# Four of 336 expert weight loads issued as sixteen transfers of eight partitions each

## What is computed

```
def moe_swiglu(h, router_w, router_b, w1, w3, w2):
    logits = (h @ router_w).astype(jnp.float32) + router_b.astype(jnp.float32)
    top_val, top_idx = lax.top_k(logits, TOP_K)
    top_p = jax.nn.softmax(top_val, axis=-1)
    combine = jnp.sum(jax.nn.one_hot(top_idx, N_EXPERTS, dtype=jnp.float32) * top_p[..., None], axis=-2)
    out = jnp.zeros_like(h)
    for e in range(N_EXPERTS):
        out = out + combine[..., e:e + 1].astype(h.dtype) * swiglu(h, w1[e], w3[e], w2[e])
    return out
```

## Time and profile before

| | us |
|---|---|
| median of 3 runs | 1876.97 (1876.92 to 1880.12) |
| profiled execution, its own time | 1879.21 |
| its span, first to last instruction | 1877.3 |
| TensorE busy (PE) | 1807.9 |
| VectorE, ScalarE, GpSimd busy | 601.2, 447.2, 409.4 |
| bytes moved by DMA | 506.40 MB |
| expert slabs issued | 336, between 987.0 and 1828.3 |
| mean granted TensorE clock | 0.992 |

### The profile page before, as it was taken

The page is one execution under the profiler, slowest core; times in us unless marked ns, Lnnn a source line. Parts: engine busy times, 40 slices in busy tenths (PEclk is TensorE's granted clock), DMA queues, the critical chain, the costliest instruction groups (busy, mean ns, idle before and its releaser), DMA issues.

```text
span 1877.3 us, 45084 instructions
## 1 busy us (share of the span) xinstructions
PE 1807.9 (96%) x20352; PEld 1325.0 (71%) x20353; DVE 601.2 (32%) x1199; ACT 447.2 (24%) x740; POOL 409.4 (22%) x126
## 2 busy tenths in 40 slices
PE   6999999999999999999999999999999889999986
PEld 4875788898888888995997566666665456666543
DVE  4356133243362454557555112021111111020112
ACT  4347423234212222527443000000000000000001
POOL 2410434445546545421552000000000000000000
PEclk8999999999999999999999999999999999999999
DMA  8352222234443474340459999999999999999993
GB/s 355 138 202 91 93 108 95 90 112 180 153 183 137 164 282 180 114 156 4 178 180 378 413 376 408 419 419 419 419 419 419 419 419 420 418 419 419 418 417 156
DMA packets 70133, 506.40 MB, mean 270 GB/s; under 512 B 7792, under 2 KB 8048, under 8 KB 9264
## 3 DMA queue, kind: packets, MB, share of 16 engines
q1 hardware_dynamic: 69552, 501.09, 66.3%
q0 software_dynamic: 384, 2.36, 0.3%
HBM read 502.37 MB, written 1.05 MB: 268 GB/s over the span
## 4 chain that ended last, share of the span: by engine, by line
PE 72%; issue 10%; DMA 6%; POOL 5%; SPq 5%; DVE 1%; ACT 1%; DVEq 0%; POOLq 0%; ACTq 0%
PE bank L1575 22%; PE bank L987 11%; PE bank L988 11%; PE bank L989 11%; PE bank L1599 9%; POOL w_lo L618 5%; SPq L845 5%; DMA moe_slab<-in_moe_w 3%; PE bank L1587 2%; DMA moe_slab<-in_moe_up 1%; DMA start_slab<-in_w_mod 1%; PE pv_bank L1338 1%; PE turned_pair L1320 1%; PE bank L1022 1%; PE bank L1296 1%
## 5 line engine op out<-in xcount | busy, mean ns | idle before, releaser
L1575 PE MATMUL bank<-moe_slab,HE 128*32 128x256 f32 x9408 | 527.3, 381 | 17.5 <-DMA moe_slab<-in_moe_up 14.2
L618 POOL TENSOR_TENSOR w_lo<-slab,w_hi 128x2048 fp32r<-128x2048 f32 (+3 forms) x88 | 369.0, 4195 | 541.2 <-ACT w_hi L1813 541.1
L1575 PEld LDWEIGHTS bank<-moe_slab,HE 128*32 128x32 f32 x9408 | 306.8, 110 | 224.8 <-DMA moe_slab<-in_moe_up 16.7
L987 PE MATMUL bank<-H_HI,w_hi 128*128 128x512 f32 (+1 forms) x912 | 321.1, 352 | 0.1
L988 PE MATMUL bank<-H_LO,w_hi 128*128 128x512 f32 (+1 forms) x912 | 319.2, 350 | 0.0
L989 PE MATMUL bank<-H_HI,w_lo 128*128 128x512 f32 (+1 forms) x912 | 319.1, 350 | 0.0
L1813 ACT ACTIVATE w_hi<-slab 128x2048 fp32r<-128x2048 f32 (+1 forms) x88 | 165.8, 1889 | 142.0 <-PE bank L989 142.0
L987 PEld LDWEIGHTS bank<-H_HI,w_hi 128*128 128x128 f32 x912 | 172.4, 189 | 26.5 <-POOL w_lo L618 1.9
L949 POOL TENSOR_TENSOR OUT<-OUT,RINVF 128x256 f32<-128x256 f32 x2 | 1.6, 813 | 864.5 <-DVE RINVF L3126 864.5
L989 PEld LDWEIGHTS bank<-H_HI,w_lo 128*128 128x128 f32 x912 | 172.5, 189 | 22.7
L988 PEld LDWEIGHTS bank<-H_LO,w_hi 128*128 128x128 f32 x912 | 172.5, 189 | 22.0
(11 more groups left out here) (316 smaller groups left out, 2123.9 us busy)
## 6 DMA issues: line engine op xcount, KB each, us to landing
moe_slab<-in_moe_up SPq DMA_DIRECT2D x224, 1024.0 KB, 26.8
moe_slab<-in_moe_w SPq DMA_DIRECT2D x112, 1024.0 KB, 27.1
slab<-in_w_in SPq DMA_DIRECT2D x38, 1024.0 KB, 4.8
slab<-in_ffn_w SPq DMA_DIRECT2D x30, 1024.0 KB, 4.8
row_slab<-in_w_mod_rows SPq DMA_DIRECT2D x28, 1024.0 KB, 7.1
start_slab<-in_w_mod SPq DMA_DIRECT2D x8, 1024.0 KB, 17.5
slab<-in_w_proj SPq DMA_DIRECT2D x8, 1024.0 KB, 4.8
slab<-in_w_out SPq DMA_DIRECT2D x8, 1024.0 KB, 4.8
```

The source lines that it names most:

```text
L618: engine.tensor_tensor(lo, raw, hi.bitcast(F32), ALU.subtract).then_inc(done, 1)
L987: mm(out, lhs[0], rhs[0], start=start, stop=False)
L1575: ins = mm(outs[t // 2][32 * b:32 * b + 32, 256 * (t % 2):256 * (t % 2) + 256], rows[t], w[:, 256 * b:256 * b + 256], start=first and t != ...
```

## The change

Slabs 84, 148, 212 and 276 are loaded as sixteen transfers of eight partitions each, one after the other, in place of one transfer of 128. All four go to buffer 4. Each of the sixteen adds 16 to the buffer's semaphore, so such a slab adds 256, and a table made beforehand, `SLAB_IN`, gives TensorE the count to wait for. `wait_expert_slab` gets the same correction. All other loads, their order and their waits stay.

```diff
--- before.py
+++ after.py
@@ -339,6 +339,14 @@
 STREAM += [("down", STEPS - 1, _i) for _i in range(2)]
 STREAM_AT = {k: n for n, k in enumerate(STREAM)}
 assert len(STREAM) == N_EXPERTS * N_EXPERT_SLABS
+
+
+SIXTEENTHS_AT = (84, 148, 212, 276)
+HOME_COUNT = [0] * MOE_RING
+SLAB_IN = []
+for _k in range(len(STREAM)):
+    HOME_COUNT[_k % MOE_RING] += 256 if _k in SIXTEENTHS_AT else 16
+    SLAB_IN.append(HOME_COUNT[_k % MOE_RING])
 
 
 
@@ -661,11 +669,12 @@
 
         def wait_expert_slab(eng, k, i):
 
-            eng.wait_ge(moe_in[k % OVER_RING], i * (16 * ROUNDS) + 16 * (STREAM_ROUNDS - N_EXPERTS * ROUNDS + k // OVER_RING + 1))
+            home = k % OVER_RING
+            eng.wait_ge(moe_in[home], i * (16 * ROUNDS) + HOME_COUNT[home] + 16 * (k // OVER_RING + 1 - N_EXPERTS * ROUNDS))
 
         def wait_stream_slab(eng, k):
 
-            eng.wait_ge(moe_in[k % MOE_RING], 16 * (k // MOE_RING + 1))
+            eng.wait_ge(moe_in[k % MOE_RING], SLAB_IN[k])
 
         def wait_slab_used(eng, k, i):
 
@@ -836,14 +845,16 @@
                 p, g = divmod(n, GROUPS)
                 src, each = (a["moe_up"], 4) if kind == "up" else (a["moe_w2"], 2)
                 row = (each * g + i) * P
-                if p:
-                    if p not in expert_of:
-                        expert_of[p] = expert_at(p)
-                    rows = src[bass.ds(expert_of[p] * (GROUPS * each * P) + row, P), :]
-                else:
-                    rows = src[row:row + P, :]
-                sp.dma_start(moe_slab[k % MOE_RING][:].rearrange("p k n -> p (k n)"), rows)\
-                    .then_inc(moe_in[k % MOE_RING], 16)
+                if p and p not in expert_of:
+                    expert_of[p] = expert_at(p)
+                dst = moe_slab[k % MOE_RING][:].rearrange("p k n -> p (k n)")
+                n = 8 if k in SIXTEENTHS_AT else P
+                for r in range(0, P, n):
+                    if p:
+                        rows = src[bass.ds(expert_of[p] * (GROUPS * each * P) + (row + r), n), :]
+                    else:
+                        rows = src[row + r:row + r + n, :]
+                    sp.dma_start(dst[r:r + n], rows).then_inc(moe_in[k % MOE_RING], 16)
 
             wait_taken(sp, ("proj", 1, 3, 2, 1))
             for k in range(5):
```

## The result

| | before | after |
|---|---|---|
| median of 6 runs each, us | 1877.43 (1876.92 to 1880.12) | 1916.74 (1914.47 to 1919.86) |
| profiled execution, its own time | 1879.21 | 1917.51 |
| its span | 1877.3 | 1915.5 |
| last slab's matmuls end | 1857.77 | 1891.14 |

The ratio is 1.020, with a 95% interval of 1.0189 to 1.021: the change costs 39 us. It was forecast to save 5.

What follows compares the result with a forecast made beforehand. The last DMA landing was taken to bound the end: late half 1845.8, early half's last engine up to 1850.9, plus 0 to 0.6 for reports, so 4.9 us earlier. 1877.0 - 4.9 = 1872.1 us, range 1869 to 1895.

Steps and rivals of the forecast that it cites:

- The bound: Whole kernel: the end follows the last slab landing one for one; delays in between are forgotten below 30.4 us of TensorE waits.
- Eight engines for a piece: DMA of a piece: eight packets of 8 KB occupy eight engines at most; 448 more packets under 512 B if so.
- Reports: DMA engines: 60 more small packets on each of eight engines, nothing to 10 ns each, up to 0.6 us in all.
- Issues on SyncE: SyncE queue: 64 issues for 4, sixteen taking 8.3 us, hidden under 26.9 us of transfers ahead, so no cost.
- rival E: DMA queue: it counts transfers, not packets, so pieces displace whole slabs and the late half runs dry; +6 us, 1883; chance 0.07.
- Late half: 1855.75 - 10.0: End of the stream: the eight late engines take no pieces and finish 10.0 us sooner, at 1845.8.
- rival C: DMA engines: the pieces take the late half, moving the last landing 4 x 2.50, +10 us, to 1887; chance 0.12.
- Full rate for a piece: DMA beside the four slabs: a slab in pieces takes 5.0 us on its eight engines, 2.50 us more than before.
- rival B: Early half takes the pieces but eight neighbouring partitions share ways into memory, slowing writes; +13 us, 1890; chance 0.22.
- 14.9 us of lead: End of the stream, under rival B: the early half's last engine finishes that far ahead of 1855.75, absorbing part of the loss.
- C with sharing: Pieces take the late half and also share ways into memory: up to +30 us; left out of the range.
- land 5 us or more late: Sign of rival B: slabs 84, 148, 212, 276 and those behind come 5 us or more late; TensorE waits after each.

## Why the prediction was wrong

*The bound: right.* The end follows the last landing one for one. It moved by 33.4 us and the end of the last slab's matmuls by 33.4. In between little is forgiven: 6.6 of 7.2 us arrive from the single slab, 23.8 from the four early ones.

*Eight engines for a piece: right,* by the 448 reports. *Reports: right as far as tested.* Eight pieces on their own ways cost nothing that can be read (-0.8 us at the last matmul, 64 reports a slab, half of the change's 128).

*Issues on SyncE: right in itself, with a consequence missed.* In the run of the lower half and in that of the copies the four stretches stay at 419 and 420 GB/s, so the issues are covered. In the changed kernel the cover breaks at slabs 212 and 276. As I read it, SyncE stands blocked on a queue that slow engines keep full, while the eight engines without pieces use up what they have. SyncE's queue in the changed kernel around slab 276 (start, length), and the windows beside it:

```profile
1699.07 19.83 SPq L857 DMA_DIRECT2D moe_slab<-in_moe_up  x19
```

```profile
1710.00:1715.00 5.00, 5.00 (x97) 2.97 (x92) 2.64 (x9) 0.00 (x0) 0.00 (x0) 1.00 0.76 274
1715.00:1720.00 5.00, 5.00 (x100) 3.00 (x96) 1.20 (x3) 0.55 (x2) 0.00 (x0) 1.00 0.54 162
```

A share of 0.54 is nearly half of the engines with nothing to do. It is part of rival E's picture, for another reason than a count of transfers. It didn't set the end: it hit engines that had 10 us to spare.

*"Late half: 1855.75 - 10.0", first failed step.* The sum took it that all eight late engines take no piece. Six don't, two do. For the two, the 2.50 us of bytes a slab come on top of 1855.75 and are not taken from it: +10.0 by the sum, +11.0 measured with the copies. With full rate everywhere the change would have ended at rival C's 1887, not at 1872. The prediction wrote that no view names the engines, and then leaned on the order of raw records. It had given C 0.12 for a question that stood open.

*Full rate for a piece, second failed step.* This is rival B, whose mechanism the runs bear out: engines that write ways in that belong to others. Its size: I took 7 us more on a slab, bytes included. Measured, the last landing moved 8.35 us a slab in the mean of four (6.6 for slab 84 alone). By the sum of the windows that is 2.5 of bytes and 23.2 / 4 = 5.8 of slow packets (10.0 + 23.2 = 33.2 against 33.4). So the price was 1.35 us short on a slab, some 5 in all. Two things in B were further off. It subtracted 14.9 us of lead, which the two late engines don't have; and it let only the engines that meet on a way lose, while the packets of 0.51 to 0.57 us at 244 GB/s show all sixteen slowed. The Trainium skill describes such a thing ("DMA: Bandwidth & Descriptors", section "Back-pressure in remote DMA"): a saturated port backs up the path, also for engines that only share the path. It says so of transfers between cores. The windows here look like it within one core, though no row names the path.

*The sum with both steps mended:* 4 x (2.5 + 5.8) = +33.2 at the last landing, 1877 + 33 = 1910. That it meets 33.4 so closely is in part luck. The same sum from the same four windows gives 34.6 against 32.7 for the second profile of the changed kernel, 26.0 against 28.1 for eight pieces of sixteen neighbours, 20.4 against 17.9 for the upper half, and 29.7 against 38.3 for the two halves, where it fails. (The last three add no bytes on the two late engines.) The median stood at 1916.7, the second set at 1915.8 against 1879.3 (+36.5). In the first profiled execution the difference of 38.3 us is 33.4 of landing and 4.9 of a long tail; the second had 32.7 and 0.1. What is left of the medians' difference, some 3 to 6 us, fits with more long tails after the change than before, but I have only a tail here and there in a profile, so that stays open.

*The range.* C with sharing was priced in the prediction at up to +30, 1907, and left outside. That is what came, and a little more: the two rivals were weighed as alternatives, when nothing stopped them from holding together.

*What the prediction would have shown it by:* it said that under B slabs 84, 148, 212 and 276 and those behind them land 5 us or more late and TensorE waits after each. The first is in the trace: slab 85 lands at 1226.6 in place of 1218.4, slab 149 at 1398.9 in place of 1381.9. The second holds for two of the four. TensorE stands idle for 4.4 us from 1220.0 and for 4.2 us from 1565.4, behind slabs 84 and 212. Beside 148 and 276 it waits for no slab, and is busy for 34.94 of 35 us and for 40.00 of 40. The last landing moved all the same. It said that the share would stand at 0.50 for longer under C. It stands at 0.14 for 12 us, because only two engines are late takers.

*Open.* Why the price on a slab is what it is. Two engines to a way for the bytes of half a slab (the sixteen engines on the lower half) should leave eight ways idle for 1.25 us more than before. By its windows (367, 392, 394 and 393 GB/s) it lost 3.1, 2.3, 2.4 and 2.5 us of stream, twice that. The two halves lost 6.0, 7.4, 8.6 and 7.7 us, where sharing alone gives 2.5, and even these leave 8.6 of their 38.3 us unaccounted for. Sharing a way costs more than its bytes, and no run says by what rule. Sixteen engines that write their own partitions in small transfers were not tried either, since one transfer takes its partitions at one fixed step and this set has none.

## What to carry to other kernels

A load of 128 partitions in one transfer is worth more than its packet count: its engines stay out of each other's way, by the split that the runs fit. If it must be cut, cut along the partitions that each engine has anyway (here eight engines, partitions 0 to 63, four apart: free; the upper half was not tried this way, on its own engines), and read the rate beside the share, since a DMA share of 1.0 at 244 GB/s instead of 419 is the sign that this has gone wrong. And before bytes are moved from late engines to early ones, measure which are late: a few extra copies within main memory, as in the run with the bytes alone, show it at the end of the stream.

## What the runs showed that I had not expected

- Eight small transfers can slow all sixteen engines to about half rate, the eight that carry none included: 220 GB/s for 5 us beside the upper pieces, with no packet of 8 KB under 0.54 us.
- Two transfers of 64 partitions cost nearly as much as sixteen of eight: by medians against the same runs of before +29.1 and +36.5 us, four slabs each.
- The late half of the engines is not a half by number: six of the engines that take no piece and two of those that do.
- The stretch behind the last landing took 26.4 and 21.6 us in two executions of the same program, with TensorE's mean granted clock at 0.67 and 0.84 there.
- A slab that lands late costs at the end also where TensorE doesn't wait beside it: four early ones cost 23.8 us.
